# Matrix-memory heads 1 to 3: value projection interleaved in quarters with the backward state steps

## The reference, cut to what matters

```
q, k = silu(dwconv(z_q)), silu(dwconv(z_k)) / sqrt(128)      # 4 taps along the tokens
v = z_v                                                     # projection alone
C_loc = einsum('l,ld,le->de', w, v, k)                      # local state of each chunk
C = a * C + s * C_loc                                       # scan over the chunks, once forward, once backward
h = (S v + wi * C0 q) / max(|den|, exp(-m))                 # output of a chunk, for both directions
```

## Time and profile before

| | |
|---|---|
| median of 3 runs | 2623.77 us (2618.14 to 2625.45) |
| span of the profiled execution | 2619.4 us |
| time of the profiled execution outside its span | not recorded |
| PE busy | 2459.3 us (94%), 14636 matmuls |
| DVE busy | 1748.3 us (67%) |
| ACT busy | 1050.9 us (40%) |
| POOL busy | 606.9 us (23%) |
| mean granted clock of TensorE | 0.978 of full speed |
| chain that ended last | PE 67%, issue 14%, DVE 9%, ACT 6% |

### The profile page before, as it was taken

One profiled execution on the slowest core, in us unless ns is written; L12 is line 12 of the kernel. 1 busy time (PEld: TensorE's weight loads), 2 busy tenths in 40 slices (PEclk: granted clock), 3 DMA queues, 4 the chain that ended last, 5 costly groups with the idle time before them and its releaser, 6 DMA issues.

```text
span 2619.4 us, 39469 instructions
## 1 busy us (share of the span) xinstructions
PE 2459.3 (94%) x14636; PEld 1353.7 (52%) x14636; DVE 1748.3 (67%) x3086; ACT 1050.9 (40%) x2078; POOL 606.9 (23%) x511
## 2 busy tenths in 40 slices
PE   7888989998899999989997899999999999999997
PEld 2444656554667868676453344444444444444443
DVE  6850535678868656556577888888896655556575
ACT  3844444376543423333444544444423322222212
POOL 0408535200000000022235443444441000000020
PEclk9999999999899999999998899999999999999999
DMA  7404323100100000130254444444528533333322
GB/s 233 127 22 140 100 79 93 25 25 9 27 20 19 18 18 18 34 106 25 73 186 135 167 165 169 143 151 156 177 85 292 186 105 98 108 101 102 99 74 65
DMA packets 176455, 260.26 MB, mean 99 GB/s; under 512 B 21320, under 2 KB 90952, under 8 KB 175608
## 3 DMA queue, kind: packets, MB, share of 16 engines
q1 hardware_dynamic: 171656, 240.95, 29.1%
q0 software_dynamic: 4608, 16.78, 2.0%
HBM read 179.18 MB, written 78.50 MB: 98 GB/s over the span
## 4 chain that ended last, share of the span: by engine, by line
PE 67%; issue 14%; DVE 9%; ACT 6%; DMA 2%; POOL 2%; SPq 0%; DVEq 0%; POOLq 0%; ACTq 0%
PE pb L2953 20%; PE pb L3052 16%; PE pb L329 12%; PE pb L2938 3%; PE pb L3067 3%; PE pb L2888 2%; DVE arena L2381 1%; PE pb L2565 1%; POOL MS L1720 1%; PE pb L338 1%; PE pb L295 1%; DVE arena L2463 1%; PE pb L2770 1%; DMA arena<-w2x 1%; PE pb L2663 1%
## 5 line engine op out<-in xcount | busy, mean ns | idle before, releaser
L2953 PE MATMUL pb<-arena 128*128 128x512 f16 (+2 forms) x2760 | 594.4, 377 | 29.2 <-DVE arena L2429 19.0
L3052 PE MATMUL pb<-arena 128*128 128x512 f16 x2352 | 513.2, 379 | 1.1 <-DVE arena L2463 0.5
L2953 PEld LDWEIGHTS pb<-arena 128*128 128x128 f16 x2760 | 268.6, 99 | 350.3 <-issue 32.9
L329 PE MATMUL pb<-arena 128*128 128x512 f16 (+1 forms) x1944 | 413.8, 375 | 13.3 <-DVE arena L1924 4.5
L3052 PEld LDWEIGHTS pb<-arena 128*128 128x128 f16 x2352 | 229.2, 98 | 280.8 <-DVE arena L2463 6.1
L2463 DVE SCALAR_TENSOR_TENSOR arena<-pb,arena 128x512 f32<-128x512 f32 x432 | 293.0, 685 | 47.5 <-PE pb L3052 24.6
L329 PEld LDWEIGHTS pb<-arena 128*128 128x128 f16 x1944 | 191.8, 99 | 233.1 <-issue 21.0
L1547 ACT ACTIVATE pb<-pb 128x512 f32<-128x512 f32 x192 | 111.7, 582 | 222.1 <-DVE pb L2434 121.1
L338 PE MATMUL pb<-arena 128*128 128x128 f16 x2880 | 173.2, 221 | 6.8 <-ACT arena L1318 4.9
L338 PEld LDWEIGHTS pb<-arena 128*128 128x128 f16 x2880 | 168.2, 99 | 9.5 <-ACT arena L1318 5.1
L1749 POOL TENSOR_TENSOR arena<-arena 128x1024 f32<-128x1024 f32 x32 | 80.6, 2541 | 216.6 <-DMA arena<-in_mlp_w 216.6
(11 more groups left out here) (359 smaller groups left out, 3883.1 us busy)
## 6 DMA issues: line engine op xcount, KB each, us to landing
w1x<-arena SPq DMA_DIRECT2D x112, 256.0 KB, 2.1
arena<-w1x SPq DMA_DIRECT2D x112, 256.0 KB, 2.7
w2x<-arena SPq DMA_DIRECT2D x106, 256.0 KB, 2.1
arena<-w2x SPq DMA_DIRECT2D x106, 256.0 KB, 2.9
arena<-in_x SPq DMA_DIRECT2D x128, 128.0 KB, 4.0
arena<-in_ada_rest POOLq DMA_DIRECT2D x32, 512.0 KB, 4.0
arena<-in_mlp_w SPq DMA_DIRECT2D x64, 256.0 KB, 6.3
arena<-in_mlp_w SPq DMA_DIRECT2D x16, 1024.0 KB, 5.7
```

The costliest lines, as they stand in the source:

```text
L329: mm = pe.matmul(pb[:, bank(jb, b), 0:n], whl[:, (i + 1) % 2, KT * ws + k, :], hT[:, k, hs, t0:t0 + n], start=(k == 0 and m == 0), stop=(k ...
L2953: mm = pe.matmul(pb[:, up_bank(pas, s, j), c], (lo if ws else hi)[:, k, :], token_op(b, L // 2, c)[:, k, hs, :], start=(k == 0 and m == 0) ...
L3052: mm = pe.matmul(pb[:, 4 + at % 4, :], left[:, hs, P * tt:P * tt + P], right[:, ws, :], start=(e == 0 and m == 0), stop=(e == 1 and m == 2))
```

## The change

In heads 1 to 3, value blocks 2, 1 and 0 are no longer projected as wholes (block 2 ahead of the backward steps, the others after steps 5 and 9). Each is cut into its four groups of 24 matmuls, and after each `csum` of the steps x = 0 to 11 PE projects one of them (`value_chunk`): block 2 in steps 0 to 3, block 1 in 4 to 7, block 0 in 8 to 11. The matmuls are the same ones. ACT evicts the three blocks after `kw` of the steps 4, 8 and 12. The split of the next head's key weight (heads 1 and 2) moves on ACT and DVE from after step 10 to after the state step of the first forward chunk, n = 0. Head 0 stays as it was.

```
# ACT
-                if h:
-                    values(h, 2)
                 act.wait_ge(S("m_silu"), 2 * h + 2)
...
                 for x in range(17):
                     kw(ITS * h + x, BWD[x], 12)
-                    if h and x in (6, 10):
-                        values(h, 1 if x == 6 else 0)
-                    if x == 10:
-                        split_hi(act, (jv if h else jq)["i"] + 2)
+                    if h and x in (4, 8, 12):
+                        values(h, 3 - x // 4)
+                    if h == 0 and x == 10:
+                        split_hi(act, jq["i"] + 2)
...
                     if n < NT - 1:
                         kw(ITS * h + 19 + n, n, 8)
-                    if h == 0 and n == 6:
-                        split_hi(act, J["q1"]["i"])
+                    if n == (6 if h == 0 else 0):
+                        split_hi(act, J["q1"]["i"] if h == 0 else jv["i"] + 2)
# DVE
-                    if x == 10:
-                        split_lo(dve, (jv if h else jq)["i"] + 2)
+                    if h == 0 and x == 10:
+                        split_lo(dve, jq["i"] + 2)
...
                         state(i0 + 19 + n, CF[n % 2], CF[(n + 1) % 2], 0, n)
+                    if h and n == 0:
+                        split_lo(dve, jv["i"] + 2)
# PE
                 if h:
-                    project(pe, jv, (4, 3, 2))
+                    project(pe, jv, (4, 3))
...
+                def value_chunk(b, q):
+                    u = unit(jv, b)
+                    if q == 0:
+                        pe.wait_ge(S("p_ev"), u - 1)
+                    for kt in range(KT):
+                        for m, (ws, hs) in enumerate(((0, 0), (1, 0), (0, 1))):
+                            c0 = BLK * b + P * q
+                            mm = pe.matmul(pb[:, bank(jv, b), P * q:P * q + P], hT[:, kt, hs, c0:c0 + P], whl[:, (jv["i"] + 1) % 2, KT * ws + kt, :],
+                                           start=(kt == 0 and m == 0), stop=(kt == KT - 1 and m == 2))
+                    if q == 3:
+                        mm.then_inc(S("p_mm"), 1)
...
                     csum(i0 + x, seq[x])
-                    if h and x in (5, 9):
-                        project(pe, jv, [1 if x == 5 else 0])
+                    if h and x < 12:
+                        value_chunk(2 - x // 4, x % 4)
```

## The result

The changed kernel takes 2636.76 us in the median of four runs (2632.62 to 2638.82) against 2620.95 for the kernel before (2615.74 to 2625.45, four runs): a ratio of 1.0059, 95% interval 1.0045 to 1.0072, so 12 to 19 us slower.

What follows compares the result with a forecast made beforehand. The queries' chain on ACT and DVE sets the start of the backward steps, then PE alone bounds them. 7.0 - 0.5 + 6.7 + 2.2 = +15.4 us on 2619.4, with 4.4 carried along: 2639, range 2629 to 2648.

Steps and rivals of the forecast that it cites:

- start of the steps, heads 2 and 3: Before the first csum: an earlier transpose frees kw a little, gaining 0.25 us in each head, 0.5 in all.
- backward steps at full clock: First csum to heads(0): 22.9 us a head with the quarters in the steps; +2.0, +2.0 and +3.0, in all +7.0 us.
- half clock after the hole: First quarters after PE's idle 6 to 6.7 us: clock falls to half, costing 2.2 us a head, 6.7 in all.
- forward chunks, the split and their clock: First forward chunk, heads 1 and 2: DVE's split delays weights(1) and heads(2), 1.1 us a head, 2.2 in all.
- the second rival: After the backward steps' tail: half clock there may go away, returning up to 1.5 us a head; 2635 us, chance 0.15.
- That the hole costs no clock: Rival, PE's idle ahead of the steps: the clock stays at full, so +8.7 us, 2632.5; chance 0.15.
- quarters cost something by themselves: Rival, backward steps: evictions or semaphore turns leave 0.2 us at each of 36 quarters, +7 more, 2646 us; chance 0.07.
- The faster rival: Start of the backward steps: PE's value blocks, not the queries' chain, set the first kw; 2617 us, chance 0.03.

Runs made afterwards that it cites:

- e2: Changed kernel plus 96 extra matmuls on PE ahead of the backward steps in heads 1 to 3, filling the hole; ratio 1.0031 to the kernel before.
- e3: Changed kernel with value block 2 whole again ahead of the steps, only blocks 1 and 0 in quarters (steps 0 to 7); ratio 0.9969 to the kernel before.
- e4: As e3, but the 192 matmuls of blocks 1 and 0 go in twelve pieces of 16, in steps 0 to 11; ratio 0.9976 to the kernel before.
- e1: Kernel before, with only the split of the next keys' weight moved to the first forward chunk (heads 1 and 2); ratio 0.9995 to the kernel before.
- e6: Changed kernel with only its split moved to the seam between the backward steps and chunk 0; ratio 1.0062 to the kernel before.

## Why the prediction was right, by its steps

It forecast 2639, +15.4 us; the ratio says +15.5, with an interval of 12 to 19. Between the first `csum` of head 1 and `heads(3)` of head 3 the two profiled executions differ by (1179.96 - 852.56) - (1167.65 - 855.11) = 14.86 us, and the measured terms make up that sum. Behind `heads(3)` of head 3 the changed kernel's execution is 1.0 us shorter, and that closes the account with the two spans (-2.55 + 14.86 - 1.00).

| term | forecast | measured |
|---|---|---|
| start of the steps, heads 2 and 3 | -0.5 | -0.40 |
| backward steps at full clock | +7.0 | +7.3 (e2 against before) |
| half clock after the hole | +6.7 | +6.98 (changed against e2) |
| forward chunks, the split and their clock | +2.2 | +0.99 |

That the forecast and the ratio agree to 0.1 us is luck: the largest term in doubt, the clock, varies by 2 us between executions (6.98 and 5.0), and the split was forecast 1.2 too high while the steps and the clock were 0.6 too low. What holds beyond luck is the mechanism: where the time goes in and why.

- **The start** did not move with block 2: the queries' chain set it, in all three heads. What gave the small gain in heads 2 and 3 was not what I wrote. I put it down to the transpose; it was ACT's eviction of block 2, which stood in ACT's list ahead of `kw`. Head 2 before and in e2, where the transpose comes as late but nothing is evicted:

```profile
992.36 2.29 DVE L2158 SCALAR_TENSOR_TENSOR arena<-arena 128x2048 f32<-128x2048 f32 x1 [0.84 <-ACT arena L1401]
...
994.25 0.39 PE L2833 MATMUL pb<-ident,arena 128*128 128x128 f32 x2
994.45 0.60 ACT L1318 ACTIVATE arena<-pb 128x512 f32<-128x512 f32 x1 [2.12 <-PE pb L338]
994.95 0.62 ACT L1413 ACTIVATE arena<-pb,CC 128x128 f32<-128x128 f32 x2
```

```profile
995.68 2.29 DVE L2156 SCALAR_TENSOR_TENSOR arena<-arena 128x2048 f32<-128x2048 f32 x1 [0.84 <-ACT arena L1401]
...
997.58 0.39 PE L2840 MATMUL pb<-ident,arena 128*128 128x128 f32 x2
998.01 0.62 ACT L1411 ACTIVATE arena<-pb,CC 128x128 f32<-128x128 f32 x2 [2.36 <-DVE arena L2156]
```

Before, `kw` starts at 994.95, 0.30 us behind the SiLU's end at 994.65, with an eviction of 0.60 us from 994.45 in its way. In e2 the transpose is at 997.58, only 0.39 us before the SiLU's end (997.97), and `kw` starts 0.04 us behind it.
- **The steps** were right to 0.1 us a head. The waits they cover are real, and e3 and e4 collect them; in the changed kernel they are 3.3 us a head in heads 1 and 2 and 2.3 in head 3 (20.87 and 19.87 less 22.96 - 5.36), against a block of 5.36 that had been free.
- **The clock** was right in cause, shown by e2, and near in size, the latter partly by luck. The spread, 1.5 to 2.9 us between heads that have the same hole within a microsecond, is as wide as in the earlier trace rows. The forecast took the mean of the two holes shown there; all four of before were followed by 6.0, 5.9, 3.0 and 5.1 us at half clock, which would have made it 7.5 us. One and the same hole isn't followed by the same stretch twice either. The hole ahead of 716.9, in code that the edit doesn't touch, was followed by 3.0 us at half clock before, and by 6.1 in the changed kernel's execution:

```profile
707.00:711.80 4.80, 0.02 (x1) 0.02 (x1) 3.00 (x8) 4.80 (x20) 0.55 (x1) 0.92 0.00 0
711.80:717.90 6.10, 6.10 (x20) 3.56 (x21) 0.00 (x0) 1.44 (x8) 0.00 (x0) 0.50 0.18 24
```

- **The split** was the term that was mis-sized: 1.1 us a head forecast, 0.74 and 0.12 measured (and 0.13 in head 3, which has no split). Its price at full clock is 1.2 (e1 and e6), but in the kernel before the clock stood at half in the same place in heads 1 and 2. In head 1 both have it; in head 2 the fall was gone in this execution, as the second rival had it for single heads, and gave back about a microsecond. Whether it falls there differs from one execution and head to the next (granted clock from `heads(0)` to `heads(3)` of head 1: 0.85 before, 1.00 in e1, 0.74 in e2, 1.00 in e4), and head 0 has it or not with the same code; so no part of the change can be said to cause it.
- **The rivals.** That the hole costs no clock would have been 7 us faster than measured, and e2, which has that clock, is that case: 8.1 us slower than before where the rival's sum said 8.7. That quarters cost something by themselves is out: 1.34 us from instruction to instruction. The faster rival asked for a SiLU before PE was done with block 3; it came 6.5 us later.

e3 gives a second reading of the edit: what was wrong is the place of block 2. With that block left where it was and the quarters of the other two in the loop, the kernel is 8 us faster than before instead of 15 slower.

## What to carry to other kernels

Work that fills another chain's latency is free only where it stands; before moving it into a loop with small waits, compare the waits that it can cover there (2.3 to 3.3 us a head) with what it covered (5.4), and look at what starts the loop. Add to the price of a new hole on PE the half clock after it, here as much as the hole's own net cost. To cover a latency between steps, take pieces just long enough (in e4 16 matmuls covered it without a wait, as 24 did) from work that is in the loop already.

## What the runs showed that I had not expected

96 useless matmuls in each hole of PE make the changed kernel faster, by 7.3 us for 288 of them in e2, since the clock then stays at 2.4 GHz for the work behind the hole. And a place where the clock is low anyway hides a part of a cost on DVE: the same split costs 1.2 us at full clock (2.42 to 3.62) and about 0.8 where PE was slow in both kernels (3.41 to 4.19 in head 1, at granted clocks of 0.52 and 0.71); that is one execution of each, so the 0.8 is rough.
